# Start of a two-layer decoder kernel: norm weights spread by 128-row products, loaded behind a memset from another queue

## The reference

```python
def rmsnorm(x, g):
    xf = x.astype(jnp.float32)
    y = xf * lax.rsqrt(jnp.mean(xf * xf, axis=-1, keepdims=True) + EPS)
    return (y * g.astype(jnp.float32)).astype(x.dtype)

p = hn @ w_in          # hn = rmsnorm(x, ln1_g[0])
```

## Time and profile before

| | |
|---|---|
| median of 3 runs | 1404.75 us (1403.91 to 1405.1) |
| the profiled execution | 1405.93 us, its span 1404.0 us |
| TensorE busy | 1390.9 us, 99% of the span |
| VectorE, ScalarE, POOL busy | 480.2, 301.8, 143.0 us |
| DMA | 462.68 MB, mean 330 GB/s |
| mean granted TensorE clock | 0.998 |

### The profile page before, as it was taken

How to read it: one execution, slowest core, us unless ns; L and a number is a source line. 1 busy time by engine, 2 the same in 40 slices (tenths; PEclk the granted TensorE clock), 3 DMA queues, 4 the chain that set the end, 5 groups by cost and what they waited for, 6 DMA issues and landing times.

```text
span 1404.0 us, 33688 instructions
## 1 busy us (share of the span) xinstructions
PE 1390.9 (99%) x15479; PEld 851.4 (61%) x15479; DVE 480.2 (34%) x794; ACT 301.8 (21%) x425; POOL 143.0 (10%) x167
## 2 busy tenths in 40 slices
PE   9999999999999999999999999999999999999997
PEld 7988999999999973363353353354354344344344
DVE  6787776776778663110110110110110110110121
ACT  6554454444645430000000000000000000000000
POOL 2660000000464000000000000000000000000000
PEclk9999999999999999999999999999999999999999
DMA  9764556665565539999999999999999999999994
GB/s 330 253 204 158 180 180 214 206 223 180 184 199 196 196 136 391 416 418 419 417 418 419 415 419 411 410 419 414 413 420 408 416 420 409 411 420 409 421 419 188
DMA packets 132012, 462.68 MB, mean 330 GB/s; under 512 B 8532, under 2 KB 66546, under 8 KB 117539
## 3 DMA queue, kind: packets, MB, share of 16 engines
q1 hardware_dynamic: 126290, 449.87, 82.4%
q0 software_dynamic: 2448, 7.94, 1.5%
q10 hardware_dynamic: 3136, 2.75, 0.6%
HBM read 455.68 MB, written 4.86 MB: 328 GB/s over the span
## 4 chain that ended last, share of the span: by engine, by line
PE 97%; DVE 2%; issue 0%; POOL 0%; ACT 0%; POOLq 0%; DVEq 0%
PE banks L1658 95%; PE banks L1849 1%; PE banks L1693 0%; DVE w_lo L830 0%; DVE mem L1109 0%; POOL ors L1611 0%; PE banks L1770 0%; DVE mem L866 0%; DVE mem L1146 0%; ACT mem L681 0%; PE banks L1951 0%; PE banks L1805 0%; PE banks L1882 0%; DVE mem L1139 0%; DVE xt L873 0%
## 5 line engine op out<-in xcount | busy, mean ns | idle before, releaser
L1658 PE MATMUL banks<-mem 128*32 128x448 f32 (+2 forms) x11712 | 878.4, 462 | 0.1
L1658 PEld LDWEIGHTS banks<-mem 128*32 128x32 f32 (+1 forms) x11712 | 381.5, 110 | 494.8 <-issue 377.5
L1658 PE MATMUL banks<-xt,w_hi 128*128 128x256 f32 (+1 forms) x1104 | 277.2, 330 | 0.0
L1494 DVE TENSOR_TENSOR mem<-mem,banks 128x448 f32<-128x448 f32 x48 | 26.9, 617 | 716.4 <-PE banks L1658 716.4
L830 DVE TENSOR_TENSOR w_lo<-mem,w_hi 128x1024 fp32r<-128x1024 f32 x178 | 222.3, 1272 | 65.8 <-ACT w_hi L559 64.4
L1658 PE MATMUL banks<-xt,w_lo 128*128 128x256 f32 x832 | 227.4, 273 | 0.0
L559 ACT CAST w_hi<-mem 128x1024 fp32r<-128x1024 f32 x178 | 182.9, 1046 | 125.9 <-PE banks L1658 123.9
L1658 PEld LDWEIGHTS banks<-xt,w_hi 128*128 128x128 f32 x1104 | 188.5, 190 | 15.4 <-issue 0.3
L1658 PEld LDWEIGHTS banks<-xt,w_lo 128*128 128x128 f32 x832 | 159.7, 192 | 0.2
L778 ACT ACTIVATE mem<-banks 128x448 f32<-128x448 f32 x48 | 22.7, 545 | 403.7 <-PE banks L1658 403.7
L1658 PE MATMUL banks<-w_hi,xt 128*128 128x512 f32 (+1 forms) x320 | 91.9, 364 | 0.6 <-DVE xt L1152 0.4
(11 more groups left out here) (225 smaller groups left out, 624.4 us busy)
## 6 DMA issues: line engine op xcount, KB each, us to landing
mem<-in_eg_dram SPq DMA_DIRECT2D x128, 896.0 KB, 13.7
mem<-in_eu_dram SPq DMA_DIRECT2D x128, 896.0 KB, 13.5
mem<-in_ed_dram SPq DMA_DIRECT2D x112, 1024.0 KB, 15.6
mem<-in_w_in_dram SPq DMA_DIRECT2D x38, 1024.0 KB, 5.5
mem<-in_fg_dram SPq DMA_DIRECT2D x11, 1024.0 KB, 5.4
mem<-in_fu_dram SPq DMA_DIRECT2D x11, 1024.0 KB, 5.4
mem<-in_fd_dram SPq DMA_DIRECT2D x11, 1024.0 KB, 4.9
mem<-in_w_br_dram SPq DMA_DIRECT2D x8, 1024.0 KB, 5.5
```

The lines of the kernel that those rows point to most:

```text
L1494: nc.vector.tensor_tensor(h, h, by_pair(bank[3 + g]), ALU.mult).then_inc(ehf_done, 1)
L1658: return nc.tensor.matmul(out, lhs, rhs, start=first, stop=last, skip_group_check=True)
```

## The change

The row of norm weights is no longer loaded first by SP. VectorE clears all of `gain` (128 by 1024) behind the memset of `zeros`, then raises `gain_cleared`; ScalarE's queue waits for it and issues the load of the row, ahead of ScalarE's first square. The ones now fill 128 rows (`all_ones`) and are set behind the clearing of `gain`, ahead of `keys` and `gates`. The two spreading products have all 128 rows as operands (rows 1 to 127 of the moving one are zeros). The first `keep_warm` has six products of zeros, not three, and so has the one ahead of the first `value_pass`. On VectorE `scaled(0, 3)` moves from behind the split of piece 2 to behind that of piece 1, ahead of `turned_low(0, 2)` and `turned_low(0, 1)`.

```diff
-        one_row = carve(3072 + DEPTH * KT * RANK, P)[0:1, :]
+        all_ones = carve(3072 + DEPTH * KT * RANK, P)
...
-        gain_in, gain_spread = sem("gain_in"), sem("gain_spread")
+        gain_in, gain_spread, gain_cleared = sem("gain_in"), sem("gain_spread"), sem("gain_cleared")
...
-            sp.dma_start(gain[0:1, :], ln1_d[0:1, :]).then_inc(gain_in, 16)
             sp.dma_start(x[:, 0, :], x_d[0, 0:P, :]).then_inc(x_in[0], 16)
...
                 if l == 0:
+                    act.wait_ge(gain_cleared, 1)
+                    act.dma_start(gain[0:1, :], ln1_d[0:1, :]).then_inc(gain_in, 16)
                     norm_squares(0, (0,))
...
             nc.vector.memset(zeros[:, :].bitcast(F32), 0.0).then_inc(init_done, 1)
+            nc.vector.memset(gain[:, :], 0.0).then_inc(gain_cleared, 1)
+            nc.vector.memset(all_ones, 1.0).then_inc(init_done, 1)
             nc.vector.memset(keys[:, :, :], 0.0)
             nc.vector.memset(gates[:, :, :], 0.0)
-            nc.vector.memset(one_row, 1.0).then_inc(init_done, 1)
...
                     until(2)
+                    scaled(0, 3)
                     turned_low(0, 2)
                     turned_low(0, 1)
-                    until(3)
-                    scaled(0, 3)
                     until(4)
...
             pe.wait_ge(init_done, 1)
-            keep_warm(3)
+            keep_warm(6)
             pe.wait_ge(init_done, 2)
             pe.wait_ge(gain_in, 16)
             for h in range(2):
-                ins = nc.tensor.matmul(bank[6 + h][:, :], one_row, gain[0:1, 512 * h:512 * h + 512], start=True, stop=True)
+                ins = nc.tensor.matmul(bank[6 + h][:, :], all_ones, gain[:, 512 * h:512 * h + 512], start=True, stop=True)
                 ins.then_inc(gain_spread, 1)
             keep_warm(2, bank[3])
...
                 if l == 0:
-                    keep_warm(3, bank[3])
+                    keep_warm(6, bank[3])
                 value_pass(base, 0, 0, 8 * l)
```

## The result

The changed kernel is slower: 1406.87 us median of 22 runs (1405.42 to 1408.92) against 1404.47 for the kernel before (22 runs, 1403.59 to 1405.33). The forecast was 1403.7 with a range of 1402.4 to 1406.2: it was wrong in direction, and the result lies outside the range. The profiled execution took 1407.07 us, its span 1405.3.

A forecast was written before the change was run, and what follows sets the result against it. TensorE, busy 99%, was taken as the bound, so early microseconds reach the end. M shifts of -0.8, -1.9 or -0.6 us by clock case gave -1.1: 1404.8 against the profiled 1405.93, median 1403.7, range 1402.4 to 1406.2.

The forecast's parts named there:

- V: When the loaded norm weights can be used and their spreading starts; taken as 4.2 us, bounds 3.9 and 7.5.
- part 1: Weights' load moved from SP to ScalarE behind the memset: x up to 0.40 us earlier, memset 0.91 us under cover.
- (b): Rival: the clock rises early but the row waits behind piece 0, V = 5.6; -0.3 us, 1404.4; chance 0.25.
- M: Start of the value product with piece 0 and the second 128 tokens; 14.72 us before, forecast 13.9 at V = 4.2.
- rival (c): Late weights hold VectorE at scaled(0,1), TensorE waits; at V = 7.5 +2.5 us, 1407.2; chance 0.10.
- X: ScalarE's start on the second x half; 7.40 us before, forecast about 7.0.
- part 5: Six zeros instead of three ahead of the first value product: 0 at 2.4 GHz, +1.28 us at 1.2 GHz.
- rival (d): The 128 rows do nothing for the clock while the added zeros do; same M as the forecast, sharing its 0.50.
- Rival (a): TensorE's clock rises where it did, about 12.5 us; M = 15.9, +1.2 us, 1405.9; chance 0.15.
- The forecast's own clock: TensorE's clock up at the end of the spreading (7.8 us); with V = 4.2, M = 13.9, -0.8 us.
- The floor of M = 12.8: Earliest M whatever V: set by the second x half's norm and VectorE's pieces, x 0.40 us earlier; -1.9 us.

The follow-up runs named there:

- e5: The changed kernel with both sets of zeros set back from six to three; median 1406.88 us, ratio 1.0019 to the kernel before.
- e10: The kernel before with six zeros ahead instead of three, nothing else; median 1405.34 us, ratio 1.0006.
- e11: The kernel before with six zeros instead of three ahead of the first value product, nothing else; median 1404.52 us, ratio 0.9999.
- e7: The kernel before with only scaled(0,3) moved to its new place; median 1404.48 us, ratio 1.0000.
- e2: e1 with the two spreading products fed by one row instead of 128; median 1406.41 us, ratio 1.0015 to the kernel before.
- e12: e9 with the spreading products fed by 32 rows instead of 128; median 1407.09 us, ratio 1.0015 to the kernel before.
- e1: The changed kernel with the row issued by SP behind the first x half, after the memset wait; median 1405.06 us, ratio 1.0003 to the kernel before.
- e9: The changed kernel with the row broadcast to 32 rows from ScalarE's queue without wait, 96 cleared, six zeros behind the spreading; median 1404.04 us, ratio 0.9997.
- e6: e9 with the broadcast load issued from SP ahead of x instead of from ScalarE's queue; median 1404.39 us, ratio 1.0000 to the kernel before.
- e3: The kernel before with only six and six zeros and the new place of scaled(0,3); median 1406.24 us, ratio 1.0010.
- e8: The kernel before with the row issued first from ScalarE's queue, without memset or wait; median 1404.53 us, ratio 1.0000.

## Why the prediction was wrong

**The wrong step is V in part 1.** The prediction took V = 4.2, "where the first x half lands", with bounds 3.9 and 7.5, because "only x and piece 0 are in front". Measured: 6.86, near the upper bound. The step that failed is the wait of the row in the DMA engines, which it had at 2.2 us from issue to use and which took 4.8. At 2.09 SP had also issued the second x half (1.64), and the row's packet started only at 6.19, when parts of that half were about to land. The load of small, issued behind 10 us, which I had set aside as the farther row, was the nearer guide: it too was issued while the engines were full. The Trainium skill (DMA: Bandwidth & Descriptors, Queues, rings and completion order) has a DMA engine take turns between queues a whole packet at a time; the prediction had weighed this as a rule that puts V at 5.6. The trace goes in that direction and further: 1.48 MB of the other queue moved between the row's issue and its first packet, nearly three transfers, where the rule, as I had read it, let the row in after piece 0.

**The way from V to M held, where V is late.** The working gave M = V + 9.7 at the low clock; 6.86 + 9.7 = 16.56, measured 16.38, and for e5 16.40 against 16.68. What happened is the mechanism of rival (c), which had a chance of 0.10: VectorE stands at scaled(0,0) and (0,1), piece 0 and 1 queue behind. V lies between the 5.6 of (b) and the 7.5 of (c). The +2.5 us priced at V = 7.5 is +1.7 at 6.86 by M, and 2.4 in the medians. The profiled execution of before was itself 1.46 above its median, so the difference of the two profiles understates the loss.

**The other terms.** The memset took 0.91 us as worked out. On VectorE it hid under the wait for x; the row's issue waited for it, though, and it stands in the chain. The removed SP issue let the first x half in at 4.17 instead of 4.63; but X was 7.81, not 7.0, and over all kernels it lies anywhere from 6.89 to 8.31: the 0.40 us is inside this scatter. The added zeros ahead were hidden in the changed kernel, as said, and bought nothing (e5). With an early row and one-row products they cost 0.9 us by the median (e10), where the prediction had 1.2. The zeros of part 5 cost nothing (e11), the new place of scaled(0,3) nothing (e7). Against rival (d), that the 128 rows do nothing for the clock, speak e2's profile and median; e12's median says that the rows matter, not that it is by the clock. Rival (a), a rise at the old time, didn't occur in the profiled execution: the clock rose at 3.92, fell at 7.33 behind the idle 2.9 us, and was back at 10.75. The forecast's own clock, up for good from the end of the spreading (7.8), was not there either. But it is not what set the time: e5, with no rise before 10.79, takes as long.

**Why the versions with an early row gain nothing either.** The floor of M = 12.8 rested on X = 7.0. The measured floor is X + 5.98, and X is 6.9 to 8.3, so M = 12.9 to 14.3. Before's median of 1404.47 less the mean offset of 1390.3 gives an estimate of M near 14.2 for its typical run (13.3 to 14.6 with the offsets seen). By that estimate the kernel before usually stands within about a microsecond of its floor already. Its profiled execution was one with a late clock (12.47, against 9.46 to 11.99 in the three others with the same work so far), and part of what I saw to be gained in it was the luck of that execution.

## What to carry to other kernels

A small load that everything waits for must be issued no later than the large ones, and another queue doesn't spare it that: moved behind a 0.9 us memset, it started only behind nearly three transfers of 0.5 MB. If a clearing must come first, clear a part that the load doesn't touch, so that the load needs no wait. And when a start depends on a clock that rises early or late, take the median of some ten runs: the one profile of before showed a late start, and that of e12 an early one, which their medians don't have.

## What was not expected of the hardware

- A 4 KB row, alone on its queue, took 4.6 us from issue to landing in the chain (2.09 to 6.72), while 1.48 MB moved on another queue, most of it issued before the row; issued 1.4 us sooner on the same queue, it was in use by 2.63.
- Behind six products of zeros the granted clock rose at 3.9 to 4.3 us in the profiles of the changed kernel, e1, e2, e9, e10 and e12, at 5.72 in e6, and only at 10.46 in e3. It fell again to 0.50 at 7.33 (changed kernel), 7.54 (e2) and 7.74 (e10), and not in e1, e6, e9 and e12.
- With the same work on TensorE up to 8.9 us, it rose anywhere from 9.46 to 12.47 (e7, e11, e8, before).
- Spreading products with 32 rows instead of 128: nearly the same durations (1.98 and 1.95 us for four), but 8 of 11 runs some 3 us longer.
- With zeros of full height and hardly a gap (TensorE idles 0.23 us ahead of the spreading), e9's runs keep within 0.7 us; those of e12, which differs in the rows alone, spread over 4.4.
